# Late modulation products of a transformer block: from one VectorE reduction per weight block to TensorE products in batches

## The reference

```
mod   = silu(c) @ w_mod + b_mod                   # w_mod is 1024 x 6144
mod_c = silu(c_ctx)[None, :] @ w_mod + b_mod
sh1, sc1, g1, sh2, sc2, g2 = split(mod, 6)
h  = modulate(rms_norm(x, norm1_w), sh1, sc1)
hc = modulate(rms_norm(ctx, norm1_w), sh1c, sc1c)
aq, ak, av, mq, mk, mv, mo, mg, ga, gm = split_in_proj(h @ w_in)
...                                               # attention, mLSTM, merge
x_mid = x + g1 * y
x = x_mid + g2 * conv_ffn(modulate(rms_norm(x_mid, norm2_w), sh2, sc2), w_up, conv_w, conv_b, w_down)
```

## Time and profile before

| what | before |
|---|---|
| median of three runs | 1361.05 us (1360.38 to 1361.74) |
| profiled execution | 1361.74 us |
| its span | 1359.9 us |
| mean granted TensorE clock | 0.964 |
| TensorE busy | 1291.7 us, 95% |
| VectorE busy | 794.4 us, 58% |
| ScalarE busy | 630.0 us, 46% |
| GpSimd busy | 697.3 us, 51% |
| read from memory | 206.35 MB, 153 GB/s over the span |

### The profile page before, as it was taken

How to read it: one execution, slowest core, us unless ns; L and a number is a source line. 1 busy time by engine, 2 the same in 40 slices (tenths; PEclk the granted TensorE clock), 3 DMA queues, 4 the chain that set the end, 5 groups by cost and what they waited for, 6 DMA issues and landing times.

```text
span 1359.9 us, 25057 instructions
## 1 busy us (share of the span) xinstructions
PE 1291.7 (95%) x9360; PEld 1178.9 (87%) x9360; DVE 794.4 (58%) x1434; ACT 630.0 (46%) x1081; POOL 697.3 (51%) x296
## 2 busy tenths in 40 slices
PE   5879999999999899999899999899999999899999
PEld 1668889886689899999887767899999999899998
DVE  3988366435551467776646642477776523677775
ACT  3622233244553565555634522555555545555553
POOL 1545463252237655556585302355558688355564
PEclk9879999999999999999898967899999999999999
DMA  9666562131125535556463200255556466355552
GB/s 376 236 232 212 212 201 77 48 97 59 48 63 171 155 140 185 184 174 218 128 186 116 86 16 30 91 190 184 179 177 224 137 188 192 112 181 177 180 181 86
DMA packets 57740, 208.47 MB, mean 153 GB/s; under 512 B 6576, under 2 KB 7600, under 8 KB 57408
## 3 DMA queue, kind: packets, MB, share of 16 engines
q1 hardware_dynamic: 57168, 205.55, 45.2%
q0 software_dynamic: 496, 1.87, 0.3%
HBM read 206.35 MB, written 1.05 MB: 153 GB/s over the span
## 4 chain that ended last, share of the span: by engine, by line
PE 88%; DVE 5%; ACT 3%; DMA 2%; issue 2%; SPq 0%; DVEq 0%; ACTq 0%
PE ps L468 23%; PE ps L469 22%; PE ps L470 22%; PE ps L683 2%; DMA raw<-in_stream 2%; PE ps L498 2%; PE ps L500 2%; PE ps L501 2%; PE ps L531 1%; PE ps L778 1%; PE ps L997 1%; PE ps L752 1%; PE ps L905 1%; PE ps L767 1%; PE ps L665 1%
## 5 line engine op out<-in xcount | busy, mean ns | idle before, releaser
L309 POOL TENSOR_TENSOR wlo<-raw,whi 128x1024 fp32r<-128x1024 f32 x284 | 691.5, 2452 | 624.5 <-ACT whi L1128 623.1
L468 PE MATMUL ps<-Hh,whi 128*128 128x256 f32 (+2 forms) x1976 | 581.8, 294 | 28.1 <-ACT arena L1206 9.6
L469 PE MATMUL ps<-Hl,whi 128*128 128x256 f32 (+2 forms) x1976 | 572.1, 290 | 0.0
L470 PE MATMUL ps<-Hh,wlo 128*128 128x256 f32 (+2 forms) x1976 | 571.7, 289 | 0.0
L468 PEld LDWEIGHTS ps<-Hh,whi 128*128 128x128 f32 (+1 forms) x1976 | 385.2, 195 | 43.0 <-issue 14.6
L1128 ACT ACTIVATE whi<-raw 128x1024 fp32r<-128x1024 f32 x338 | 353.0, 1052 | 112.8 <-DMA raw<-in_stream 42.2
L469 PEld LDWEIGHTS ps<-Hl,whi 128*128 128x128 f32 (+1 forms) x1976 | 386.0, 195 | 2.9
L470 PEld LDWEIGHTS ps<-Hh,wlo 128*128 128x128 f32 (+1 forms) x1976 | 385.6, 195 | 2.6
L1972 DVE SCALAR_TENSOR_TENSOR arena<-ps,sm,arena 128x255 f32<-128x255 f32 (+1 forms) x264 | 127.2, 482 | 106.2 <-ACT arena L1376 98.2
L468 PE MATMUL ps<-dh,whi 128*128 128x256 f32 x592 | 168.3, 284 | 5.4 <-DVE wlo L1948 3.0
L470 PE MATMUL ps<-dh,wlo 128*128 128x256 f32 x592 | 168.2, 284 | 0.0
(11 more groups left out here) (294 smaller groups left out, 1294.9 us busy)
## 6 DMA issues: line engine op xcount, KB each, us to landing
raw<-in_stream SPq DMA_DIRECT2D x386, 512.0 KB, 4.3
X<-in_xc SPq DMA_DIRECT2D x2, 1024.0 KB, 10.4
out_y<-X SPq DMA_DIRECT2D x8, 128.0 KB, 2.0
kx<-in_const POOLq DMA_DIRECT2D x1, 512.0 KB, 6.9
arena<-in_wgate POOLq DMA_DIRECT2D x1, 400.0 KB, 8.9
params<-in_params POOLq DMA_DIRECT2D x1, 372.0 KB, 6.9
k<-in_const POOLq DMA_DIRECT2D x1, 256.0 KB, 4.8
kx<-in_const POOLq DMA_DIRECT2D x1, 256.0 KB, 4.3
```

The lines of the kernel that those rows point to most:

```text
L309: pool.tensor_tensor(wlo[:, slot, :], raw[:, rslot, :], whi[:, slot, :].bitcast(f32), ALU.subtract).then_inc(rest_done[0], 1)
L468: pe.matmul(out, lh, rh, start=start, stop=False, skip_group_check=True)
L469: pe.matmul(out, lh, rl, start=False, stop=False, skip_group_check=True)
L470: return pe.matmul(out, ll, rh, start=False, stop=stop, skip_group_check=True)
```

## The change

The late modulation products move from VectorE to TensorE.

- The host now lays M16 to M47 out like the early ones: four sections (g1, sh2, sc2, g2) of eight blocks, each 128 inputs by 1024 outputs of one section.
- `mod_batch` on TensorE multiplies four blocks at a time. A block is four products of 256 columns, each on its own group of 32 columns of the array and its own 32 partitions of bank 3. Eight blocks add up into one section.
- The batches stand behind jobs 1, 2, 3, 5, 7, 9, 11 and 13. In the stream the four blocks of a batch stand together, three weight blocks later than the job (behind w4, w5, w6, w8, w10, w12, w14, w16).
- ScalarE copies each finished section into a free part of X at q = 2, 5, 9 and 13, behind `evac(q)` and its splits. The first product of section 1, 2 or 3 waits for the copy of the section before.
- After job 15 TensorE turns the four sections with eight transposes, and VectorE adds the bias in two instructions (`modb_add`). Job 18 waits for them.
- `c_across`, its eight broadcast matmuls and the products `late_mods` are gone. `raw` slots of late blocks are freed by TensorE (`mod_used`).

```diff
-MODS_BEHIND = [0] * S_BRANCH
-for _s in range(2, 28):
-    MODS_BEHIND[_s] = 1
...
+MOD_BATCHES = [(q, q + 3, 4) for q in (1, 2, 3, 5, 7, 9, 11, 13)]
+SECT_AT = (2, 5, 9, 13)
@@ sync: load
-                    if kind == "mod" and n < MOD_FIRST:
+                    if kind == "mod":
                         sp.wait_ge(mod_used, n + 1)
-                    elif kind == "mod":
-                        sp.wait_ge(mod_sum, n - MOD_FIRST + 1)
@@ splittable
-            made = mods_upto(max(q + MOD_LEAD, MODS_AHEAD))
+            made = MOD_FIRST + sum(count for at, _, count in MOD_BATCHES if at <= q)
@@ tensor
-                    for c in range(KC):
-                        mm = pe.matmul(PS[:, 3 + c // 4, P * (c % 4):P * (c % 4) + P],
-                                       c_cols[:, c, 0:1].broadcast_to((P, P)), ident, start=True, stop=True)
-                    mm.then_inc(S["c_bc"], 1)
+            def mod_batch(count):
+                for n in range(mods[0], mods[0] + count):
+                    sect, k = divmod(n - MOD_FIRST, KC)
+                    if k == 0 and sect > 0:
+                        pe.wait_ge(S["sect_out"], sect)
+                    r = RAW_OF_MOD[n]
+                    wait_raw(pe, r)
+                    for j in range(4):
+                        mm = pe.matmul(PS[32 * j:32 * j + 32, 3, T * (sect % 2):T * (sect % 2) + T], c_cols[:, k, :],
+                                       raw[:, r % RING, T * j:T * j + T], start=k == 0, stop=k == KC - 1)
+                    mm.then_inc(mod_used, 1)
+                mods[0] += count
+            def mod_turns():
+                pe.wait_ge(S["sect_out"], 4)
+                pe.wait_ge(S["ut_ready"], 1)
+                for sect in range(4):
+                    for half in range(2):
...
+                mm.then_inc(S["sect_t"], 1)
                     if q == AV:
-                        pe.wait_ge(S["ut_ready"], 1)
+                        pe.wait_ge(S["modb_done"], 2)
+                for at, _, count in MOD_BATCHES:
+                    if at == q:
+                        mod_batch(count)
+                if q == 15:
+                    mod_turns()
@@ scalar
-            act.activation(c_across, PS[:, 3:5, :].rearrange("p b n -> p (b n)"), ACT.Copy)\
-               .then_inc(S["c_across"], 1)
+                if q in SECT_AT:
+                    sect = SECT_AT.index(q)
+                    act.wait_ge(mod_used, MOD_FIRST + KC * (sect + 1))
+                    act.activation(X[:, sect, T:2 * T], PS[:, 3, T * (sect % 2):T * (sect % 2) + T], ACT.Copy)\
+                       .then_inc(S["sect_out"], 1)
@@ vector
-            def late_mods(upto):
-                for n in range(mods[0], upto):
-                    r, at = RAW_OF_MOD[n], n - MOD_FIRST
-                    wait_raw(dve, r)
-                    dve.scalar_tensor_tensor(raw[:, r % RING, :], raw[:, r % RING, :], 1.0, c_across,
-                                             ALU.mult, ALU.mult, accum_out=MODB[:, at:at + 1]).then_inc(mod_sum, 1)
+                if q == 16:
+                    dve.wait_ge(S["sect_t"], 1)
+                    for b in range(2):
+                        modb_add(b)
-                late_mods(mods_upto(q + MOD_LEAD))
```

More of the change, by code:

```diff
@@ L35 @@
 MOD_FIRST = 2 * KC
-MOD_LATE = 4 * KC
 GM0 = W_IN_JOBS.index("gm")
-MODS_BEHIND = [0] * S_BRANCH
-for _s in range(2, 28):
-    MODS_BEHIND[_s] = 1
[L41 to L44, removed]
+MOD_BATCHES = [(q, q + 3, 4) for q in (1, 2, 3, 5, 7, 9, 11, 13)]
+SECT_AT = (2, 5, 9, 13)
 STREAM = [("mod", n) for n in range(MOD_FIRST)]
@@ L48 @@
     STREAM.append(("w", _s))
-    STREAM += [("mod", _n + _i) for _i in range(MODS_BEHIND[_s])]
-    _n += MODS_BEHIND[_s]
+    for _, _behind, _count in MOD_BATCHES:
+        if _behind == _s:
+            STREAM += [("mod", _n + _i) for _i in range(_count)]
+            _n += _count
 STREAM += [("w", s) for s in range(S_BRANCH, S_END)]
@@ L53 @@
 RAW_OF_MOD = {n: r for r, (kind, n) in enumerate(STREAM) if kind == "mod"}
-def mods_upto(s):
-    return MOD_FIRST + sum(MODS_BEHIND[:s + 1])
 FFN_STARTS = (S_FFN1, S_FFN2, S_FFN3)
@@ L208, in build @@
         mod_rows = ar(A_MO + 512, 512)
-        c_across = ar(A_MO + 4 * T, D)
         ROWJ = sb("junk", [P, T], mybir.dt.bfloat16)
@@ L223, in build @@
         mod_used = sem("mod_used")
-        mod_sum = sem("mod_sum")
         s_out = sem("out_written")
@@ L243, in build @@
             "sb_arg", "sb_wm", "fox_max", "fox_pt", "fox_even", "t2_lo", "mix_cu", "fin", "wg_lo",
-            "spread_ready", "v_chain", "rot_fin", "rows_read", "c_across", "modb_done",
-            "c_bc", "mod_t", "mod_copy", "ss_ready", "gates_ps", "u_t", "st_done", "bc_done", "qk_done", "pv_done", "rot_done", "rstd_bc", "sc_done",
+            "spread_ready", "v_chain", "rot_fin", "rows_read", "sect_out", "modb_done",
+            "sect_t", "mod_t", "mod_copy", "ss_ready", "gates_ps", "u_t", "st_done", "bc_done", "qk_done", "pv_done", "rot_done", "rstd_bc", "sc_done",
             "tr_done", "av_done", "recip_bc", "t_ps", "gates2_ps", "fin_bc", "z_done", "r_done", "sbv_done", "fs_done",
@@ L556, in _ @@
             mm.then_inc(S["mod_t"], 1)
+            mods = [MOD_FIRST]
+            def mod_batch(count):
[15 more added lines that the diff above has]
+                    for half in range(2):
+                        at = P * (2 * (sect % 2) + half)
+                        mm = pe.transpose(PS[:, 2 + sect // 2, at:at + P], X[:, sect, T + P * half:T + P * half + P],
+                                          ident)
+                mm.then_inc(S["sect_t"], 1)
             pe.wait_ge(S["wg_lo"], 1)
@@ L1177, in _ @@
             rsqrt_start(0)
-            act.wait_ge(S["c_bc"], 1)
-            act.activation(c_across, PS[:, 3:5, :].rearrange("p b n -> p (b n)"), ACT.Copy)\
-               .then_inc(S["c_across"], 1)
             splits_upto(1)
@@ L1215, in evac @@
                     if q == MO:
-                        act.wait_ge(mod_sum, MOD_LATE)
+                        act.wait_ge(mod_used, 6 * KC)
                     if q == MO + 1:
@@ L1399, in ffn @@
                 splits_upto(f + 3 * NF + 3)
-            act.wait_ge(S["modb_done"], 1)
             norm(1, lambda u: MODB[:, 8 + u:9 + u])
@@ L1618, in norm, with modb_add @@
                                                      ALU.add, ALU.subtract).then_inc(S["hl_done"], 1)
-            mods = [MOD_FIRST]
-            def late_mods(upto):
-                for n in range(mods[0], upto):
-                    r, at = RAW_OF_MOD[n], n - MOD_FIRST
-                    wait_raw(dve, r)
-                    dve.scalar_tensor_tensor(raw[:, r % RING, :], raw[:, r % RING, :], 1.0, c_across,
-                                             ALU.mult, ALU.mult, accum_out=MODB[:, at:at + 1]).then_inc(mod_sum, 1)
-                mods[0] = max(mods[0], upto)
+            def modb_add(b):
+                turned = PS[:, 2 + b, :].rearrange("p (s h j r) -> p s j h r", s=2, h=2, j=4)
+                dve.tensor_tensor(MODB[:, 16 * b:16 * b + 16].rearrange("p (s j h) -> p s j h", s=2, j=4),
+                                  turned[:, :, :, :, 0], pr("b_mod", 16 + 16 * b, 32 + 16 * b)
+                                  .rearrange("p (s j h) -> p s j h", s=2, j=4), ALU.add).then_inc(S["modb_done"], 1)
             first_norm()
             gains_of_queries()
-            dve.wait_ge(S["c_across"], 1)
-            late_mods(mods_upto(MOD_LEAD))
             dve.wait_ge(S["gates_ps"], 1)
@@ L1642, in _ @@
             link(dve.memset(bb, 0.0))
-            late_mods(mods_upto(MODS_AHEAD))
             dve.wait_ge(S["gate_act"], 3)
@@ L1715, in _ @@
             rotated(9)
-            dve.wait_ge(mod_sum, MOD_LATE)
-            dve.tensor_tensor(MODB[:, :], MODB[:, :], pr("b_mod", 2 * KC, 6 * KC), ALU.add).then_inc(S["modb_done"], 1)
             def make_spread(to, first, blocks, n=16):
@@ L2236, in layout @@
     first = w_mod[:, 0:2 * D].reshape(KC, P, 2, D).transpose(0, 2, 1, 3).reshape(2 * KC, P, D)
-    mod = np.concatenate([first, w_mod[:, 2 * D:].T.reshape(4 * KC, P, D)])
+    mod = np.concatenate([first, w_mod[:, 2 * D:].reshape(KC, P, 4, D).transpose(2, 0, 1, 3).reshape(4 * KC, P, D)])
     rows = np.concatenate([np.arange(HD * h, HD * h + HD) for h in order])
```

## The result

| | before | changed |
|---|---|---|
| median | 1360.72 us (4 runs, 1360.01 to 1361.74) | 1379.45 us (4 runs, 1377.38 to 1379.73) |
| span of the profiled execution | 1359.9 us | 1372.7 us |
| mean granted TensorE clock in it | 0.964 | 0.970 |

The change makes the kernel slower. The table's median is that of four executions; eleven were timed, from 1374.99 to 1379.73 us, with a median of 1377.38. Their ratio to before is 1.0122 (95% interval 1.0109 to 1.0137). On 1360.72 us that is 16.6 us more (14.8 to 18.6). The same kernel timed twice more gave 1.0135 (1.0118 to 1.0151) and 1.0122 (1.0107 to 1.0136). The forecast was 12.9 us.

The account below looks back on a forecast made before the run. TensorE was taken as the bound, busy 1291.7 of 1359.9 us. Added 26.6 us less 13.7 gone or hidden gave +12.9: 1374.6 from the profiled run, 1374.0 from the median; own range 1369 to 1379, wider range 1364 to 1382.

Parts of the forecast that it names:

- The wait that goes: TensorE's idle stretch from 79.9 to 89.4 us goes, 9.56 us, with the low clock behind it, 3.0 us.
- The price of a late block: On TensorE, two float32 passes of 0.22 us with four column groups side by side: 0.44 us, 14.1 for 32 blocks.
- changing form: Eight TensorE batches enter and leave the 32-column form: about 0.2 us a batch, 1.6 us in all (0 to 4).
- eight transposes: On TensorE at job 15, 8 x 0.11 us and a start: about 1 us added.
- Rival 4: The four column groups do not run side by side: 43 us on top, over 1400 us; chance 0.04.
- rival 3: Both float32 passes of all groups run together, 0.22 us a block, no new wait: -4.7 us, 1356; chance 0.05.
- The new waits: TensorE waits ahead of batch 3, job 6 and batch 7, behind ScalarE's splits: 3.9, 1.5 and 2.8, together 8.2 us.
- The clock: The 3.9 us wait can lower TensorE's clock behind it: 1.7 us taken, about half of 3.0 (0 to 5).
- 1.1 hidden: Batch 1 runs over TensorE's old small wait at 59.0 us, so 1.1 us of added work is hidden.
- landings: Transfers of weight blocks: a run's first lands 3.7 us after its slot is freed, 4.7 in a busy queue.
- nothing but a shift: Behind 200 us, no new difference: every later job just starts the same distance later, some 13 us.
- Rival 2: Slot to landing takes 5.2 to 6 us, each new wait grows: +17 to +21 us, 1378 to 1382; chance 0.12.

Follow-up runs that it names:

- b_cap: Kernel before with ScalarE's split look-ahead cut from 6 jobs to 5 for jobs 0 to 11; 1349.92 us, ratio 0.9919.
- f_one_group: Changed kernel with copy first and look-ahead 4, three of four products left out in 28 of 32 late blocks; 1365.81 us, ratio 1.0042.
- a_copy_first: Changed kernel with each section copy directly behind its evacuation, ahead of the splits; 1369.52 us, ratio 1.0070.
- a_free: Changed kernel with section copies ahead of the splits and ScalarE's look-ahead cut to 4 jobs for jobs 0 to 15; 1368.16 us, ratio 1.0053.
- a_cap: Changed kernel with only ScalarE's look-ahead cut to 4 jobs for jobs 0 to 15, copies still behind splits; 1368.0 us, ratio 1.0055.
- a_again2: Changed kernel unedited, timed and profiled again a second time; 1376.54 us, profiled span 1377.5 us.

## Why the prediction was right, and where it was short

The mechanism came out as forecast, piece by piece. The size did so less well than 12.9 against 12.8 us suggests: against all runs the forecast is 3.7 us short, and the median of the first four, 1379.45 us, lies just above the forecast's own range of 1369 to 1379.

**The wait that goes.** Forecast 9.6 + 3.0 us. It is gone from the changed kernel. Alone, in the kernel before, its removal is worth 11 us by the runs of b_cap, and 12.6 in its profile: the decay rows' product starts at 185.63 instead of 197.31 us, though job 2 started 0.9 us later (61.02 against 60.12). The wait needed two things at once, VectorE's late product and ScalarE's order. b_cap changes the order alone and VectorE keeps its products, so the order was enough to remove it.

**The price of a late block.** Forecast 0.44 us a block and 0.2 us a batch for changing form, 15.7 us for all. Measured 2.06 us a batch, 16.5 us: 0.43 us of columns a block and 0.3 us a batch around them. By the Trainium skill, TensorEngine Tiling (Array Packing), Key Properties, a change of tiling mode drains the engine; the estimate of 2.7 us for 16 such changes that the prediction gives beside its 1.6 fits the eight batches (16.5 - 13.8 = 2.7) better than the 1.6 that it used. The eight transposes (L565) cost 0.9 us, forecast 1.0. Rival 4 (groups one after another) falls by f_one_group, rival 3 (both passes together) by the 0.22 us from record to record there.

**The new waits.** Forecast ahead of batch 3, job 6 and batch 7, of 3.9, 1.5 and 2.8 us; measured 4.11, 1.26 and 3.74. The walk from landing to landing gave all three places. The single sizes are partly luck, since they change with the execution (4.1 to 5.7, 0.6 to 1.8, 2.4 to 3.7 us in three profiles); the sum, forecast 8.2, was 9.1 to 9.3 in all three. That they come from splits ahead of the copy and of the evacuation is shown by a_copy_first, a_free and a_cap.

**The clock.** Forecast 1.7 us, as one lump behind the first wait. In the first profile batch 3 lost 1.6 us by it, in a_again2 it cost about 2.6 us more than in the first. As a single number the term was about right for one execution and too small for the other.

**The sum.** In the first profile: gone 9.6 + 3.0 and 1.1 hidden; added 16.5 + 0.9 + 9.1 + 1.6 = 28.1; net 14.4. Measured at the decay rows are 14.0, or 14.5 counted from 57 us, where this execution was already 0.5 us ahead of before (the same product starts at 57.02 instead of 57.49). The forecast had 12.9. So the terms that were too small are the changes of form (1.1 us) and the waits (0.9). Behind the waits are the landings: I took 4.7 us in a busy queue; the first profile shows, from issue to landing between 57 and 100 us,

```profile
DMA to landing us min/median/max: 3.4/5.9/8.0
```

where before had a median of 5.2, and a_again2 has 6.1. Then 1.2 us come back by the clock behind 660 us, which brings the span difference to 12.8, beside the forecast. The prediction had expected nothing but a shift there.

Rival 2 (heavier waits, 1378 to 1382) had 0.12, and three of the first four timed runs lie in its range; 16.6 us for all runs is nearly its lower end of 17. Its premise, landings of 5.2 to 6 us, is what the profiles show, but its waits are not: it wanted 1 to 1.5 us more on each of the three, and their sum grew by 1. What the timed runs have above the profiled one is, where a_again2 shows it, mostly the clock; for the runs without a profile the split is open.

## What to carry to other kernels

Before moving work off an engine that a wait names, look at what stands in order on the engine between: here a look-ahead that let one in-order engine wait for a transfer with evacuations behind it cost 11 us before the change and 7 to 10 after it, and one number removed it. Work moved onto the engine that bounds the kernel costs its full price but for what falls into a wait (here about 1 of 16.5 us), and if it also consumes blocks of a shared ring it ties the stream to that engine's progress. Forecast such waits by walking from slot freed to landing to split to copy, and give the transfer its median in that stretch rather than a quicker value (here 5.2 us stood in the profile before, and 4.7 was used). And compare the forecast with many runs: two single profiles agreed with it to 0.1 us, and all runs to 3.7.

## What the runs showed of the hardware

Products of 32 columns in four column groups run side by side in float32 at 256 moving columns: 32 records take 1.93 us, 8 records 1.91 us. One pass of a block takes 0.22 us. Entering and leaving that form costs about 0.3 us a batch beyond this. A record of 2 columns in that form still takes 0.03 us. Three executions of one program differed in the clock granted behind the same waits, and the slowest had about 2.6 us of its delay from it. Loads of the same size in the same program took 3.4 to 8.0 us from issue to landing, and the same link of the chain took 6.13 us in one execution and 6.86 in another.
